# One decoder layer on one core: rows of keys turned ahead of the query, a value job begun before the channel root's spread, scores reduced by halves

## The reference

```
h = x + 0.5 * rms(ffn1(rms(x)))                       # SwiGLU, inner width 4096
z = rms(h) @ w_in;  u, v, a, gate = split(z, 4)        # each 512 wide
out_a = u * (tril(W_s) @ layer_norm(v) + b_s)          # per chunk of 128 positions, 4 heads
glu = a * sigmoid(gate);  c = causal_dwconv31(glu)     # its last 30 rows are an output
h = h + rms(concat[out_a, silu(layer_norm(c))] @ w_out)
k, v = rms(mem) @ w_k, rms(mem) @ w_v                  # 256 memory tokens, both are outputs
h = h + rms(softmax(q k^T / 16) v @ w_o)               # q = rms(h) @ w_q, 4 heads of 256
h = h + 0.5 * rms(ffn2(rms(h)))
```

## Time and profile before

| | |
|---|---|
| median of three runs | 1638.08 us (1637.2 to 1642.01) |
| profiled execution, its own time | 1636.59 us |
| span of its instructions | 1634.9 us |
| mean granted TensorE clock | 0.999 of full speed |
| TensorE busy | 1603.0 us, 98% of the span |
| VectorE busy | 1001.0 us, 61% |
| ScalarE busy | 703.5 us, 43% |
| POOL busy | 185.6 us, 11% |
| DMA | 159.06 MB, mean 97 GB/s |

### The profile page before, as it was taken

How to read it: one execution, slowest core, us unless ns; L and a number is a source line. 1 busy time by engine, 2 the same in 40 slices (tenths; PEclk the granted TensorE clock), 3 DMA queues, 4 the chain that set the end, 5 groups by cost and what they waited for, 6 DMA issues and landing times.

```text
span 1634.9 us, 28859 instructions
## 1 busy us (share of the span) xinstructions
PE 1603.0 (98%) x12062; PEld 1556.0 (95%) x12062; DVE 1001.0 (61%) x1290; ACT 703.5 (43%) x1211; POOL 185.6 (11%) x167
## 2 busy tenths in 40 slices
PE   8999999999999999999999999999999999999998
PEld 7999999999999989997999869899999999999998
DVE  4873675477367566999344442687367547637753
ACT  5551453255145444642543333555145325515543
POOL 2010220121022000000000010001022012102200
PEclk9999999999999999999999999999999999999999
DMA  5132233223232331233334442223233323322321
GB/s 177 53 104 78 82 100 104 77 84 124 62 94 89 118 112 53 78 104 113 129 108 155 155 167 91 69 62 110 72 92 90 104 78 94 114 75 82 102 80 59
DMA packets 137322, 159.06 MB, mean 97 GB/s; under 512 B 3134, under 2 KB 130706, under 8 KB 137193
## 3 DMA queue, kind: packets, MB, share of 16 engines
q1 hardware_dynamic: 131616, 138.16, 26.9%
q0 software_dynamic: 5488, 19.10, 3.4%
q10 hardware_dynamic: 96, 0.02, 0.0%
HBM read 152.22 MB, written 5.40 MB: 96 GB/s over the span
## 4 chain that ended last, share of the span: by engine, by line
PE 89%; DVE 9%; ACT 1%; issue 0%; DMA 0%; POOL 0%; ACTq 0%; DVEq 0%; POOLq 0%
PE slot L1923 43%; PE slot L2070 38%; DVE f L1715 4%; PE slot L1967 2%; PE slot L1951 1%; PE slot L2310 1%; PE slot L2329 1%; DVE f L1338 1%; PE slot L1973 1%; PE slot L1981 1%; DVE f L1722 1%; DVE wp L1308 0%; PE slot L2350 0%; PE slot L2369 0%; ACT prob L1240 0%; DVE h L1343 0%
## 5 line engine op out<-in xcount | busy, mean ns | idle before, releaser
L2070 PE MATMUL slot<-nb,wu 128*128 128x288 f32 x4704 | 631.4, 295 | 1.5 <-ACT part L891 1.5
L2070 PEld LDWEIGHTS slot<-nb,wu 128*128 128x128 f32 x4704 | 628.4, 188 | 2.0 <-ACT part L891 2.0
L1923 PE MATMUL slot<-mid,wp 128*128 128x288 f32 x3696 | 502.7, 296 | 1.8 <-DVE mid L1328 1.8
L1923 PEld LDWEIGHTS slot<-mid,wp 128*128 128x128 f32 x3696 | 494.9, 189 | 5.2 <-DVE mid L1328 3.4
L741 ACT ACTIVATE wp<-raw 128x1024 fp32r<-128x1024 f32 x104 | 109.5, 1059 | 309.1 <-PE slot L1923 280.3
L1308 DVE TENSOR_TENSOR wp<-raw,wp 128x1024 fp32r<-128x1024 f32 x104 | 127.0, 1221 | 109.6 <-ACT wp L741 109.6
L666 POOL TENSOR_TENSOR raw<-raw,q 128x512 f32<-128x512 f32 x56 | 80.9, 1445 | 829.5 <-DVE wu L1465 525.0
L1923 PE MATMUL slot<-n,wp 128*128 128x288 f32 x960 | 134.9, 298 | 1.0 <-DVE n L1328 1.0
L1923 PEld LDWEIGHTS slot<-n,wp 128*128 128x128 f32 x960 | 128.9, 189 | 4.4 <-DVE n L1328 3.8
L1616 DVE TENSOR_TENSOR f<-slot,f 128x576 f32<-128x576 f32 x48 | 36.3, 757 | 137.6 <-PE slot L1923 137.6
L1475 DVE TENSOR_TENSOR wu<-raw,wu 128x512 fp32r<-128x512 f32 x56 | 38.8, 692 | 96.0 <-ACT wu L872 96.0
(11 more groups left out here) (284 smaller groups left out, 1662.7 us busy)
## 6 DMA issues: line engine op xcount, KB each, us to landing
raw<-in_ffn_w_gate_dram SPq DMA_DIRECT2D x32, 1024.0 KB, 5.6
raw<-in_ffn_w_up_dram SPq DMA_DIRECT2D x32, 1024.0 KB, 5.6
raw<-in_ffn_w_down_dram SPq DMA_DIRECT2D x32, 1024.0 KB, 5.0
raw<-in_mix_w_in_dram SPq DMA_DIRECT2D x8, 1024.0 KB, 5.1
kring<-in_cache_mem_k_dram POOLq DMA_DIRECT2D x6, 1024.0 KB, 5.3
raw<-in_xattn_w_k_dram SPq DMA_DIRECT2D x4, 1024.0 KB, 5.3
raw<-in_xattn_w_v_dram SPq DMA_DIRECT2D x4, 1024.0 KB, 5.1
raw<-in_mix_w_out_dram SPq DMA_DIRECT2D x4, 1024.0 KB, 5.8
```

The costliest lines, as they stand in the source:

```text
L1923: ins = pe.matmul(slot(u)[:, half, 0:HALF], weights(J)[:, wi, kt], X(xi, kt, half), start=kt == 0 and k == 0, stop=kt == KT - 1 and k == l ...
L2070: ins = pe.matmul(dst[:, 0:HALF], wu[:, p, wi, kt], nb[:, p, xi, kt], start=start and kt == 0 and k == 0, stop=kt == KH - 1 and k == len(P ...
```

## The change

- In the mixing tail, one use `glu` takes the place of `glup` and `glus`: the cache rows are turned behind `cmean`, ScalarE copies them to `osm` ahead of its squares, and POOL stores them right then.
- `cvar`'s spread is issued behind the fifth of the eight products of `v4`'s first job.
- The rows of keys are turned behind `post2`'s spread instead of behind `v4`; they lie in the region of `mid`. ScalarE copies them behind its first square for `pre3`. The 16 identity products in front of `q` are left out (those of the other norms stay).
- POOL issues both stores of rows behind the first three loads of cached keys and clears `qs` as soon as the cache stores and `out` are done. ScalarE awaits the store of keys ahead of the first exponential, not ahead of `pre3`.
- VectorE makes the low parts of the first two `out` weights behind the last four low parts of `mid`.
- The scores are reduced in two halves of two heads, each with a signal of its own (`sc_half`, `mx_ready`); the exponentials of two heads wait for their half.
- The first scores wait for all but the last tile of `q`; only the last head waits for that.
- The first two jobs of `o` run as prompt half, sample turn, prompt half of the second, then the two other halves.

```diff
-    pl.use("cmean", "sg0", "sg1", "cvar", "sg2", "sg3")
+    pl.use("cmean", "glu", "sg0", "sg1", "cvar", "sg2", "sg3")
     pl.job_run("v4", 4)
-    pl.use("ktok0", "ktok1")
     pl.job_run("out", 8)
-    pl.use("vtok0", "post2", "vtok1", "glup", "glus", "pre3")
+    pl.use("vtok0", "post2", "vtok1", "ktok0", "ktok1", "pre3")
...
-                   [("vT", [P, KT, MEM], F32), ("ktok", [P, MT, D], F32)],
+                   [("vT", [P, KT, MEM], F32)],
...
-        rm = views("region_mid", [("mid", [P, PARTS, KT, T], PDT)],
+        rm = views("region_mid", [("mid", [P, PARTS, KT, T], PDT)], [("ktok", [P, MT, D], F32)],
...
+        sc_half = sem("sc_half")
...
-            for name, dst, rows, done in (("ktok", mem_k_o, ktok, k_stored), ("vtok", mem_v_o, vtok, v_stored)):
+            def store_rows(name, dst, rows, done):
                 for t in range(MT):
                     wait_freed(pool, f"{name}{t}")
-            wait_freed(pool, "glup")
+
+            wait_freed(pool, "glu")
             pool.dma_start(cs_p[0, 0, :, :], osm[64:64 + LEFT, :]).then_inc(stored, 16)
-            wait_freed(pool, "glus")
             pool.dma_start(cs_s[0, :, LEFT - DEC:LEFT, :], osm[0:NB * DEC, :]).then_inc(stored, 16)
 
...
             nc.gpsimd.memset(qs[:, :, :, :], 0.0).then_inc(qs_zero, 1)
             for b in (1, 2, 3, 0, 4, 5, 6, 7):
                 if b == 0:
+                    store_rows("vtok", mem_v_o, vtok, v_stored)
+                    store_rows("ktok", mem_k_o, ktok, k_stored)
                     pool.wait_ge(job_done, pl.base["q"][0] + 5)
                 elif b < 4:
                     pool.wait_ge(job_done, pl.base["out"][0] + 8)
...
                     nc.scalar.activation(square_of(t), h[:, t], ACT.Square).then_inc(sums[pre]["squared"], 1)
+                    if t == 0 and behind_first:
+                        behind_first()
...
+            wait_aux(act, "glu")
+            nc.scalar.activation(osm[64:64 + LEFT, :], aux("glu")[0:LEFT, 0, :], ACT.Copy)
+            free_aux(nc.scalar.activation(osm[0:NB * DEC, :], aux("glu")[0:NB * DEC, 1, :], ACT.Copy), "glu")
             for t in range(CT):
...
-            rows_turned("ktok", ktok)
...
                         if job == "out":
 
-                            act.wait_ge(stored, 16 * 3)
+                            act.wait_ge(stored, 16 * 5)
                         prepare(behind + 1)
...
-            def rows_of_mix():
-                rows_turned("vtok", vtok)
-                wait_aux(act, "glup")
-                free_aux(nc.scalar.activation(osm[64:64 + LEFT, :], aux("glup")[0:LEFT, 0, :], ACT.Copy), "glup")
-                wait_aux(act, "glus")
-                free_aux(nc.scalar.activation(osm[0:NB * DEC, :], aux("glus")[0:NB * DEC, 0, :], ACT.Copy), "glus")
-
-            project("out", "post2", rows_of_mix)
-            act.wait_ge(k_stored, 16)
-            pre_norm("post2", "pre3", "xattn_g_pre", "q", "query")
+            project("out", "post2", lambda: rows_turned("vtok", vtok))
+            pre_norm("post2", "pre3", "xattn_g_pre", "q", "query", behind_first=lambda: rows_turned("ktok", ktok))
             warm(ACT.Exp)
...
+            act.wait_ge(k_stored, 16)
             for i in range(4):
-                act.wait_ge(mx_ready, i + 1)
                 if i >= 2:
                     wait_aux(act, f"pt{i - 2}")
                 for hd in range(HEADS):
+                    if hd % 2 == 0:
+                        act.wait_ge(mx_ready, 2 * i + hd // 2 + 1)
                     ins = nc.scalar.activation(prob[:, i % 2, hd], aux(f"sc{i}")[:, hd // 2, (hd % 2) * MEM:(hd % 2 + 1) * MEM],
                                                ACT.Exp, bias=mx[:, 4 * i + hd:4 * i + hd + 1],
                                                accum_out=sm[:, 4 * i + hd:4 * i + hd + 1])
...
             wait_freed(dve, "cvar")
             for t in range(CT):
                 V.tensor_tensor(f[:, 4 + t], f[:, 4 + t], R[:, :], ALU.mult).then_inc(cn_ready, 1)
-            for t in range(2):
-                prepare(pl.base["out"][0] + t)
             for t in range(CT):
                 dve.wait_ge(mid_hi, HI0["mix"] + 4 + t + 1)
                 V.tensor_tensor(mid[:, 1, 4 + t], f[:, 4 + t], mid[:, 0, 4 + t].bitcast(F32), ALU.subtract)\
                     .then_inc(mid_ready, 1)
+            for t in range(2):
+                prepare(pl.base["out"][0] + t)
...
             for i in range(4):
-                wait_aux(dve, f"sc{i}")
-                V.tensor_reduce(mx[:, 4 * i:4 * i + 4], flat(aux(f"sc{i}")).rearrange("p (h m) -> p h m", h=HEADS),
-                                AX_X, ALU.max, negate=True).then_inc(mx_ready, 1)
+                for half in range(2):
+                    if half == 0:
+                        dve.wait_ge(sc_half, i + 1)
+                    else:
+                        wait_aux(dve, f"sc{i}")
+                    V.tensor_reduce(mx[:, 4 * i + 2 * half:4 * i + 2 * half + 2],
+                                    aux(f"sc{i}")[:, half, :].rearrange("p (h m) -> p h m", h=2),
+                                    AX_X, ALU.max, negate=True).then_inc(mx_ready, 1)
...
-            def memory_jobs(name, count):
+            def memory_jobs(name, count, between=None):
...
                     for kt in range(KT):
                         ins = pe.matmul(slot(u)[:, 0, 0:MEM], raw[:, s % RAW, kt, (J % 2) * P:(J % 2 + 1) * P], memT[:, kt, :],
                                         start=kt == 0, stop=kt == KT - 1)
+                        if between and i == 0 and kt == 4:
+                            between()
                     ins.then_inc(job_done, 1)
...
                 wait_slot(pe, u)
-                for i in range(16):
+                for i in range(0 if pre == "pre3" else 16):
                     pe.matmul(slot(u)[:, 0, 0:P], ident[:, :], ident[:, :], start=True, stop=True)
...
                 pe.wait_ge(conv_step, 2 * (t // 2 + 1) * TAPS)
                 pe.wait_ge(taps_added, t + 1)
                 sum_tile("cmean", t, CT, f[:, 4 + t])
+
+            for e in range(4):
+                wait_use_freed(pe, pl.base["glu1"][1] + e)
+            pe.wait_ge(gs_ready, 1)
+            turn("glu", [(aux("glu")[0:LEFT, 0, ct * P:(ct + 1) * P], glu[:, ct, SEQ:SEQ + LEFT]) for ct in range(CT)]
+                 + [(aux("glu")[0:NB * DEC, 1, ct * P:(ct + 1) * P], gsm[:, ct, :]) for ct in range(CT)])
             spatial((0, 1))
             for t in range(CT):
                 pe.wait_ge(*normed_to("cvar", "squared", t + 1))
                 sum_tile("cvar", t, CT, sq[:, t % 2])
             spatial((2, 3))
-            spread_out("cvar")
-            memory_jobs("v4", 4)
+
+            memory_jobs("v4", 4, lambda: spread_out("cvar"))
...
-            for t in range(MT):
-                turn_row("ktok", kT, t)
             jobs("out", half_of(mid), lambda kt: pe.wait_ge(mid_ready, MID0["mix"] + kt + 1))
...
-            def other_rows():
-                turn_row("vtok", vT, 1)
-                for e in range(4):
-                    wait_use_freed(pe, pl.base["glu1"][1] + e)
-                turn("glup", [(aux("glup")[0:LEFT, 0, ct * P:(ct + 1) * P], glu[:, ct, SEQ:SEQ + LEFT]) for ct in range(CT)])
-                pe.wait_ge(gs_ready, 1)
-                turn("glus", [(aux("glus")[0:NB * DEC, 0, ct * P:(ct + 1) * P], gsm[:, ct, :]) for ct in range(CT)])
-
-            sum_squares("post2", first_rows, other_rows)
+            sum_squares("post2", first_rows, lambda: turn_row("vtok", vT, 1))
+            for t in range(MT):
+                turn_row("ktok", kT, t)
             jobs_normed("q", "pre3", KT)
 
-            for e in range(4):
+            for e in range(3):
                 wait_use_freed(pe, pl.base["q"][1] + 4 + e)
 
...
                 for hd in range(HEADS):
+                    if i == 0 and hd == HEADS - 1:
+                        wait_use_freed(pe, pl.base["q"][1] + KT - 1)
                     for d in range(2):
                         ins = pe.matmul(aux(name)[:, hd // 2, (hd % 2) * MEM:(hd % 2 + 1) * MEM],
                                         f[:, 2 * hd + d, i * P:(i + 1) * P], kT[:, 2 * hd + d, :], start=d == 0, stop=d == 1)
+                    if hd == 1:
+                        ins.then_inc(sc_half, 1)
...
-            J, u = start_job("o", 0)
-            for half in range(2):
+            def half_job(J, u, half):
                 for kt in range(KT):
                     if half == 0:
                         wait_freed(pe, f"pv{kt}")
-                    elif kt == 0:
-                        turn_samples()
-                        wait_freed(pe, "pvt")
                     for k, (wi, xi) in enumerate(PRODUCTS):
                         ins = pe.matmul(slot(u)[:, half, 0:HALF], weights(J)[:, wi, kt], mid[:, xi, kt, half * HALF:(half + 1) * HALF],
                                         start=kt == 0 and k == 0, stop=kt == KT - 1 and k == len(PRODUCTS) - 1)
```

(18 more changed lines are left out.)

## The result

The changed kernel takes 1627.3 us (median of four runs, 1626.22 to 1628.84), the kernel before 1638.32 (1637.2 to 1642.01): a ratio of 0.9935, 95% interval 0.9923 to 0.9947, so 10.6 us less, between 8.7 and 12.6. Six further executions of the changed kernel beside eleven of the one before gave 0.9937 (0.9922 to 0.9951). The prediction said 1628.3 us, 1625.0 to 1633.0, and faster with a chance of 0.87.

A forecast was written before the change was run, and what follows sets the result against it. TensorE, carrying 89% of the chain, was taken as the bound outside four places where it waits. 3.6 + 1.2 + 1.0 + 2.5 + 1.5 = 9.8 us took the median from 1638.08 to 1628.3, range 1625.0 to 1633.0.

The forecast's parts named there:

- Part a: Mixing tail: `cvar`'s spread moved into `v4`, no clock fall, `out` starting earlier; 3.6 us less, bounds 2.0 to 4.0.
- the hole: Mixing tail: TensorE's idle 2.03 us for the channel root's reciprocal would go, paid by 0.96 us of transposes.
- the 1.6 us of clock: Mixing tail: price of the clock's fall in `v4`'s first half, 1.6 us, taken as gone.
- Part b: `post2`: spread released by its reciprocal, no longer behind the "glus" turn; 1.2 us less, bounds 0.7 to 1.3.
- The tie of banks: `q`: its second and third jobs want banks just as the key copies free them; cost 0 to 0.5, taken 0.
- second rival: Ahead of `q`: without identity products TensorE idles 1.45 us and the clock falls there, costing 1.6 us: 1629.9; chance 0.08.
- Part c: Attention: earlier first scores (1.03 us) and no waits for the scores' bank in four rounds (2.5 us).
- part d: First `o` jobs: the second job's first half covers the 1.54 us wait; 1.5 us less, bounds 1.0 to 1.54.
- The spare microsecond: Attention: the scores' bank would come free 1.0 us before TensorE returns for it.
- a renamed wait in attention: Attention: the early half comes late, the bank still frees behind four exponentials, 2.5 us stays: 1630.8; chance 0.09.
- a double failure: The edit fails in two places, attention's wait and the mixing tail's clock, with late `out` load: gain about 4, 1634; chance 0.09.
- a clock at half throughout `q`: From `q`'s start until the tiles of `n` are through, the clock stays at half: slower, 1643.5; chance 0.04.

The follow-up runs named there:

- the eight products: Changed kernel with eight identity products (1.87 us) between `v4` and `out`; from the end of `cmean`'s sums to the first `out` product 25.83 us, 1.34 more.
- the kernel with the hole filled: Kernel before with eight identity products in TensorE's 2.03 us wait ahead of `cvar`'s spread; median 1636.35 us over ten executions against 1636.75, ratio 1.0002.
- filler: Changed kernel with four identity products (0.9 us) ahead of the last norm's single-column sums, run twice; medians 1626.26 and 1627.09 us, ratios 0.9937 and 0.9927.

## Why the prediction came out

**Part a, 3.6 forecast, 3.65 measured.** The working gave 3.71 from the first product's start before, 794.36, and took 3.6; stage A's 3.90 counts from the chain's 794.61, from which the working gives 3.96. Each step is in the trace: the transposes took 0.87 on the chain (0.96), the hole closed, `v4` ran at full clock, the second job's end released the load, and `out` started on the low part. Counted from the end of `cmean`'s sums, which came 0.41 us sooner, ahead of every edit, the load went out at 17.17 (17.03 worked out) and `out` began at 24.49 (24.43). The weights were last by 0.45 (0.4), which the eight products showed. That the keys' turns were worth 1.3 and not 1.9 was right. The part that I can't carry over is the 1.6 us of clock: right in the trace from which it was read and in one more, yet the kernel with the hole filled was no faster over ten executions, and a hole of 1.89 us went without a fall in another. As a term of the median it was taken too surely; what it is worth over executions stays open, and that the forecast of the median came so near owes something to luck there.

**Part b, 1.2 forecast, 1.26 measured.** The spread follows its reciprocal. The tie of banks cost nothing; with the copies one tile later it costs 2.3 us and, in the one trace there is, a fall of the clock with it. The prediction's second rival did not come: TensorE idled 1.66 us (1.45 worked out) with the clock at 1.00 behind it in every trace of the stage as changed. The one with the late copies shows that a fall there is possible.

**Part c, 3.5 forecast, 4.25 measured; part d, 1.5 forecast, 1.9 measured.** The mechanism was right, the terms were mis-sized: I counted the idle time in brackets alone. Undone one by one, the three edits cost 3.16, 1.27 and 1.87 us for waits of 2.7, 1.05 and 1.54. A wait costs TensorE 0.1 to 0.3 us more than it shows, since the products behind it neither overlap the end of the one before nor have their weights loaded as far ahead. The spare microsecond was there: the bank came free 0.9 us ahead of its turn (1.0 worked out), and in the third round VectorE sat idle 2.13 and 1.03 us ahead of its two reductions.

**The sum.** The stages gave 11.0 (with `out`'s 0.22) for the 9.8 forecast, nearly all of the difference from parts c and d; 10.6 is what the ratio gives. But the 11.0 holds 1.7 us of a fall that the kernel before may not have in every execution, and leaves out the last stage, which was not in my sum. In the nine traces that have the changed parts and no filler it took 13.4 us once, 15.1 five times and 16.7 three times, and in the three of the kernel before and its edit 13.4 twice and 15.1 once. Nothing of that stage was changed. Whether it falls there more often now, or the traces only met it so, is open; three traces against nine do not tell.

The rivals of a renamed wait in attention, of a double failure and of a clock at half throughout `q` did not come. None of the new waits is in the chain.

## What to carry to other kernels

Put work that depends on nothing into the wait for a small chain (a root and its reciprocal, a maximum, a split), and look at once at what is late next: here the weights' load, by 0.45 us in most traces and up to 0.93. Count a removed wait of TensorE as its idle time and 0.1 to 0.3 us on top. Check which buffers a moved copy frees: at `q` they tie with their users, and one tile later they cost 2.3 us of wait, 4.6 with the fall of the clock in that trace.

## What the runs showed that I had not expected

TensorE's clock fell from 2.4 to 1.2 GHz for 3.4 or 6.8 us at a time, up to four times in a trace of this kernel between its start and its last turns (two traces have no such fall), and not in the same places each time: behind 11 to 12 us, 601, 777, 852 (the late copies only), 1024 to 1036 and 1609 to 1616 us (1623 in the kernel before). These are, but for the start, a root with its spread, the key turns ahead of `q` and the last norm: places where TensorE waits. Most traces pass most of these places unharmed. A fall cost 1.6 to 1.7 us in the mixing tail and the last stage, where TensorE was the bound (3.2 where it lasted 6.8), and 0.2 to 0.8 us behind 1024, ahead of the second feed-forward part, where VectorE was. One trace with a fall says that a place is exposed, not what the exposure costs in the median: kernels that differ by 1.7 us in a stage of their traces had medians 0.4 us apart.

Each of these falls but one stands behind or within idle time of TensorE, from 0.8 us ahead of the last norm's sums to 3.5 us at the start, where it waits for a load. The one is the fall in the last stage of the second trace with the filler, where only the single-column products stood ahead of it. The Trainium skill ("TensorE: Matmul & The Clock Gate", section "What's actually happening") says that half rate is the default and activity lifts it; the direction of all the other falls agrees. That a fall depends on the execution as well shows in the holes of about 2 us, two with a clock of 0.65 and 0.62 in the four microseconds behind them and one with 1.00.
